# DeltaNet's q, k and v projection as seven products of halves, with weight sums by GpSimd during attention and operands streamed from DRAM

## The reference

```
def encoder_layer(x, ...):
    h = rms_norm(x, norm1_g)
    proj = h @ w_in
    q_lat, kv_lat, k_rope, qkv, z, a_f, a_b, b_f, b_b = split_cols(proj, SPLITS)
    mla_out = mla_mixer(q_lat, kv_lat, k_rope, ...)
    gdn_out = gdn_mixer(qkv, z, a_f, a_b, b_f, b_b, ...)
    x = x + jnp.concatenate([mla_out, gdn_out], axis=-1) @ w_o
    x = x + ec_moe(rms_norm(x, norm2_g), w_router, w_gate, w_up, w_down)

def gdn_mixer(qkv, z, ...):
    qkv = jax.nn.silu(centred_depthwise_conv(qkv, conv_w))      # 5 taps
    q, k, v = split_cols(qkv, (1024, 1024, 1024))               # 8 heads of 128 each
    q = l2_normalize(q); k = l2_normalize(k)
    ...                                                         # chunked delta rule, forward and backward
```

## Time and profile before

| | |
|---|---|
| median of 3 runs | 2980.59 us (2979.1 to 2981.39) |
| the profiled execution, its own time | 2983.76 us |
| its span in the trace | 2982.0 us |
| TensorE busy | 2801.7 us, 94% |
| VectorE, ScalarE, GpSimd busy | 1092.2, 609.8, 601.6 us |
| DMA | 603.95 MB, 203 GB/s on average |

### The profile page before, as it was taken

One profiled execution on the slowest core, in us unless ns is written; L12 is line 12 of the kernel. 1 busy time (PEld: TensorE's weight loads), 2 busy tenths in 40 slices (PEclk: granted clock), 3 DMA queues, 4 the chain that ended last, 5 costly groups with the idle time before them and its releaser, 6 DMA issues. The chain is left out here.

```text
span 2982.0 us, 53948 instructions
## 1 busy us (share of the span) xinstructions
PE 2801.7 (94%) x19063; PEld 1404.3 (47%) x19063; DVE 1092.2 (37%) x2185; ACT 609.8 (20%) x1806; POOL 601.6 (20%) x969
## 2 busy tenths in 40 slices
PE   8999999999999999999788999999999999999997
PEld 4544455555666666566465455432223232322232
DVE  1145444421674575476675434411111111111100
ACT  4100455412213312311411010321111111111100
POOL 1444111104214222320530000212111111112111
PEclk9999999999999999999899999999999999999999
DMA  6664100021111110200413637799999999999996
GB/s 241 220 219 132 53 29 29 11 94 57 57 44 50 44 57 24 70 23 26 147 44 146 235 141 261 290 424 408 376 400 385 398 390 398 395 387 394 378 412 216
DMA packets 170388, 603.95 MB, mean 203 GB/s; under 512 B 16527, under 2 KB 81895, under 8 KB 116455
## 3 DMA queue, kind: packets, MB, share of 16 engines
q1 hardware_dynamic: 163175, 587.58, 51.4%
q0 software_dynamic: 6912, 12.59, 2.4%
HBM read 554.14 MB, written 45.98 MB: 201 GB/s over the span
## 5 line engine op out<-in xcount | busy, mean ns | idle before, releaser
L2727 PE MATMUL psum<-wbuf 128*32 128x512 f32 x2976 | 334.9, 606 | 24.7 <-issue 22.9
L1444 PE MATMUL psum<-xT,wbuf 128*128 128x512 f32 x720 | 342.0, 613 | 0.3 <-PEq L828 0.3
L2727 PE MATMUL psum<-x,wbuf 128*32 128x512 f32 x3024 | 330.1, 592 | 0.0
L715 POOL COPY wbuf<-xT 128x16 f32 x533 | 114.4, 215 | 759.9 <-issue 433.5
L2727 PEld LDWEIGHTS psum<-wbuf 128*32 128x32 f32 x2976 | 98.4, 112 | 255.9 <-issue 255.9
L715 DVE COPY wbuf<-xT 128x16 f32 x500 | 94.4, 190 | 337.2 <-issue 336.3
L2727 PEld LDWEIGHTS psum<-x,wbuf 128*32 128x32 f32 x3024 | 99.2, 110 | 225.3 <-issue 225.3
L1444 PEld LDWEIGHTS psum<-xT,wbuf 128*128 128x128 f32 x720 | 133.3, 194 | 127.4 <-issue 122.4
L2745 PE MATMUL psum<-x,hT 128*32 128x512 f32 x1584 | 173.3, 593 | 13.9 <-DVE hT L2808 13.2
L715 ACT COPY wbuf<-xT 128x16 f32 x503 | 111.2, 221 | 276.5 <-issue 273.9
L1447 PE MATMUL psum<-xT,wbuf 128*128 128x256 f32 x736 | 164.9, 379 | 0.0
(11 more groups left out here) (330 smaller groups left out, 3694.4 us busy)
## 6 DMA issues: line engine op xcount, KB each, us to landing
x<-in_w_down SPq DMA_DIRECT2D x66, 1024.0 KB, 11.0
wbuf<-in_w_gate SPq DMA_DIRECT2D x65, 1024.0 KB, 10.3
wbuf<-in_w_up SPq DMA_DIRECT2D x65, 1024.0 KB, 12.9
x<-in_w_gate SPq DMA_DIRECT2D x63, 1024.0 KB, 8.0
x<-in_w_up SPq DMA_DIRECT2D x63, 1024.0 KB, 10.6
wbuf<-in_w_down SPq DMA_DIRECT2D x62, 1024.0 KB, 11.7
wbuf<-in_w_in SPq DMA_DIRECT2D x16, 2048.0 KB, 8.9
wbuf<-weight_sums SPq DMA_DIRECT2D x16, 2048.0 KB, 9.4
```

The costliest lines, as they stand in the source:

```text
L715: last = copy(k.xeT[:, half, :, t:t + 1], k.mixT[:, :, cols][:, :, bass.ds(r, 1)])
L1444: last = nc.tensor.matmul(ps[:, b, 0:SS_], wg[:, m % 2, d, h * P:(h + 1) * P], k.xT[:, d, SP_:T], start=(d == 0), stop=(d == KD - 1))
L2727: last = nc.tensor.matmul(ps[32 * j:32 * j + 32, g, :].rearrange("p (x n) -> p x n", x=2), xeT[:, half, q, 32 * g:32 * g + 32], m[:, :, kk ...
```

## The change

The three kinds (k, q, v) of a pair of heads become one unit of work ("kind"): two heads side by side, two halves of the tokens (384 each) and two halves of the width. Instead of 8 block products, 7 are made (Strassen's scheme). Each product has 8 steps of 384 tokens. A pair needs 21 products, 168 steps; the four pairs need 84 products, 672 steps.

* The four sums of weights per kind are formed by GpSimd in the attention block, in 48 units of three subtractions, and stored to DRAM (`qkv_weight_sums`). The four sums of tokens fall out of the z products of the first block and are stored there (`token_operands`).
* In DeltaNet the weights of a product are loaded six products ahead into six slots, and the token operands into three slots of `xT` (a fourth, A22, stays). Six of seven products need a fresh token operand of 1.5 MB, which is issued when the product that used the slot before is done.
* Products land in two PSUM banks in turn. ScalarE copies the first product of each kind out (`keep`), VectorE adds the six others into `pre` (`add`), with one or two blocks each.
* The convolution of a kind can begin when its seventh product is added; v is the last kind of a pair.
* In attention the last pair gets two steps a tile, and three products in all, in place of 40 steps.
* The z tiles are paired 0 with 3, 1 with 4, 2 with 5, and `xT` is laid out by halves of the tokens.

The core of the diff:

```
+TYPES = (1, 0, 2)
+PRODUCT_ORDER = (1, 6, 2, 7, 5, 4, 3)
+TOKENS_OF = {1: A11, 2: A12, 3: S4, 4: A22, 5: S1, 6: S2, 7: S3}
+W_SLOTS = 6
+IN_ATTENTION = 3 * HK
+def product_step(k, p, d):
+    v, _ = TOKEN_AT[p]
+    last = k.nc.tensor.matmul(k.psum[:, product_bank(p), 0:SIDE], k.w_slot[p % W_SLOTS][:, d, :],
+                              k.x_slot[v].rearrange("p (k t) -> p k t", k=HK)[:, d, :],
+                              start=(d == 0), stop=(d == HK - 1))
...
@@ attention, SyncE @@
+                def comb_load(u):
+                    n, kp = divmod(u, 4)
+                    if u >= 2:
+                        sp.wait_ge(s_cs[u % 2], cs_base + 16 * (u // 2))
+                    c0 = C_QKV + TYPES[n % 3] * GW + n // 3 * 2 * P
+                    for g in range(2):
+                        k0 = HK * g + 2 * kp
+                        src = a["w_in"][0].rearrange("(p k) n -> p k n", k=KD)[:, k0:k0 + 2, c0:c0 + 2 * P]
+                        for h in range(2):
+                            sp.dma_start(w_comb[u % 2][:, 2 * g + h], src[:, :, h * P:(h + 1) * P]).then_inc(s_cl[u % 2], 16)
+                def comb_store(lo, hi):
+                    for u in range(lo, hi):
+                        n, kp = divmod(u, 4)
+                        if u + 1 < N_COMB:
+                            comb_load(u + 1)
+                        sp.wait_ge(s_comb, comb_base + 3 * u + 3)
+                        sp.dma_start(k.wsum[n, :, :, 2 * P * kp:2 * P * (kp + 1)].rearrange("m p c -> p m c"),
+                                     w_comb[u % 2].rearrange("p m k c -> p m (k c)")).then_inc(s_cs[u % 2], 16)
+                UNITS_TO = ((5, 10, 18), (18, 23, 32), (32, 36, 44), (44, 44, N_COMB))
@@ attention, GpSimd @@
+                combine(0, 5)
                 for i in range(HP):
                     pool.wait_ge(s_sq, i * NT + NT)
...
                     nc.gpsimd.tensor_tensor(qrot[..., HALF:], tmp[:, 0], tmp[:, 1], ALU.add).then_inc(s_qr, 1)
                     pool.wait_ge(s_qr, i + 1)
+                    combine(*((5, 13), (13, 27), (27, 41), (41, N_COMB))[i])
@@ attention, TensorE @@
-                        first_qkv(3 * u, 3 * u + 3)
+                        products(min(2 * u, 2 * HK), min(2 * u + 2, 2 * HK))
@@ DeltaNet, SyncE @@
+                def refill(lo, hi):
+                    for p in range(lo, hi):
+                        if p + W_SLOTS >= N_PROD and p not in TOKEN_LOADS:
+                            continue
+                        sp.wait_ge(s_prod, PROD_BASE + p + 1)
+                        for v, o in TOKEN_LOADS.get(p, ()):
+                            load_tokens(k, sp, v, o)
+                        if p + W_SLOTS < N_PROD:
+                            load_weights(k, sp, p + W_SLOTS)
...
                     if i + 1 == HP:
-                        sp.wait_ge(s_proj, HP * NC)
+                        sp.wait_ge(s_prod, PROD_BASE + N_PROD)
+                        for n in (KINDS - 2, KINDS - 1):
+                            convolved(sp, n)
                         sp.dma_start(k.mixT[:, 0:H], k.mix[0:H].rearrange("h p t -> p h t")).then_inc(k.s_mix, 16)
@@ DeltaNet, TensorE @@
-                project(0, 1, SECOND)
-                for c in range(2, NC):
-                    project(0, c)
+                project(21 * HK - IN_ATTENTION)
...
-                            project(i + 1, c, at, at + a)
+                            project(a)
...
-                            project(i + 1, c, at + a, at + a + b)
+                            project(b)
...
-                        project(i + 1, 4, LV * sum(IN_LEVEL[2]),
-                                between={12: lambda: scan(i, 4, 0), 14: lambda: scan(i, 4, 1), 16: lambda: scan(i, 4, 2),
-                                         20: lambda: scan(i, 5, 0), 24: lambda: scan(i, 5, 1), 28: lambda: scan(i, 5, 2)})
-                        steps = {6: lambda: output(i)}
+                        project(28 - LV * sum(IN_LEVEL[2]),
+                                {0: lambda: scan(i, 4, 0), 2: lambda: scan(i, 4, 1), 4: lambda: scan(i, 4, 2),
+                                 7: lambda: scan(i, 5, 0), 10: lambda: scan(i, 5, 1), 13: lambda: scan(i, 5, 2)})
+                        steps = {12: lambda: output(i)}
...
-                        project(i + 1, 5, between=steps)
+                        project(28, steps)
@@ DeltaNet, VectorE @@
+                def add(p):
+                    n, m, q = product_of(p)
+                    dve.wait_ge(s_prod, PROD_BASE + p + 1)
+                    jobs = {6: [(kept, c21)], 2: [(c11, c21)], 7: [(c21, kept)], 5: [(c22, c21), (kept, kept)],
+                            4: [(c21, c21)], 3: [(c12, kept)]}[q]
+                    for to, of in jobs:
+                        for cols, o in to:
+                            last = nc.vector.tensor_tensor(o, ps[:, product_bank(p), cols], of[0][1][:, cols], ALU.add)
@@ DeltaNet, GpSimd @@
-                    pool.wait_ge(s_pre, m + 1)
+                    pool.wait_ge(s_ea, scalar_to(7 * kind + 6))
+                    pool.wait_ge(s_ev, vector_to(7 * kind + 6))
```

More of the change, by code:

```diff
@@ L349, in _ @@
                 comb_store(13, 18)
+                sum_store(S4, 0)
                 load_w(3)
@@ L1996, in _ @@
                                 copy_part(2)
+                        if more and r < 2:
+                            add(p0 + (8, 11)[r])
                         if r < 2:
```

459 lines of the change are left out of this document (301 added, 158 removed).

## The result

The changed kernel takes 3055.03 us (median of 4 runs, 3047.12 to 3058.71) against 2980.99 us before: ratio 1.0246, 95% interval 1.0233 to 1.0258. It is 74 us slower. The forecast was 3056 us in a range of 2992 to 3100.

What follows compares the result with a forecast made beforehand. TensorE, busy for 94% of the span, was taken to bound the kernel; 47 + (9 - 3.4) - 15 + 35 + 1 + 2 = 75.6 us, set against 2980.6, gave 3056 us, with a range of 2992 to 3100.

Steps and rivals of the forecast that it cites:

- The gain on TensorE: Projection steps: 62.0 us gross, as 12.0 in attention, 3.4 in the first projection and 46.3 in three pairs.
- What of the 46.3 is left: Three full DeltaNet pairs: 5.0 us a pair kept after waits and VectorE's additions, 15 in all, bounds 0 and 25.
- the pair's start: Start of each DeltaNet pair: 56 steps save 5.2 us, 2.0 kept because the third sum of squares waits for ScalarE.
- The additions: VectorE adding products in the DeltaNet pairs: up to 18 us a pair, 3 of it counted on the chain.
- DeltaNet's first step: Fourth product waits for S3, loaded only after the barrier behind 1.0 MB of weights: cost 9 us, bounds 6 and 13.
- The weight sums in attention: GpSimd's units, 6.2 us each, make rotations late: attention grows by 47 us net of the 12.0 gain, bounds 21 and 68.
- The rotations: Attention: rotations 0 and 1 late by about 2 us each, 2 and 3 by 26 each; sum 56, bounds 33 and 72.
- The clock: Three long waits let TensorE's clock fall, and it starts again at 1.2 of 2.4 GHz: 2 us, bounds 0 and 5.
- The last pair: Loads of `mix` and output weights wait for GpSimd's v convolution, TensorE waits 40 us: cost 35, bounds 28 and 38.
- The first block: Token sums must be stored before VectorE forms the next; the last store leaves product 6 late: 1 us, bounds 0 and 4.
- The stream: Rival: token and weight operands bind DeltaNet's products, adding 20 us, or 60 with worse queueing: 3076 to 3116; chance 0.05.
- The faster rival: Both queues keep up, under 4.6 us a unit and last pair covered: 2962, or 2925 if filling counts in full; chance 0.12.

Runs made afterwards that it cites:

- experiment 6: Changed kernel with VectorE adding only 8 columns of each block in place of up to 384; 3044.06 us, ratio 1.0222.
- experiment 2: Changed kernel with all 48 weight-sum units left out, products needing a sum reading a plain block of weights; 3004.29 us, ratio 1.0087.
- experiment 9: Changed kernel with early last-pair loads, three unit buffers, new rotation cuts and SyncE stops, S3 loaded in attention, reordered squares; 2956.2 us, ratio 0.9916.
- experiment 5: Changed kernel with each DeltaNet token operand load bringing only 128 of 3072 columns; 3042.04 us, ratio 1.0216.
- experiments 9 and 10: The second of these: experiment 9's kernel with S1 early too, product 1's weights ahead of the store of mix, later sums of squares; 2943.73 us, ratio 0.9877.

## Why the prediction was right, and where only its sum was

The sum was +75.6 us, the profiled execution has +74.8. Both large mechanisms were right and shown by taking each away. Its parts were less exact than the sum:

* **The gain on TensorE** (62.0 gross). Attention without units is 12.8 us shorter (12.0). From the first step to the last pair TensorE's busy time fell by 41.0 where 3.4 + 46.3 = 49.7 were taken out. The granted clock is 0.97 against 0.98; one hundredth of 734 us is 7, an estimate, so it can hold most of the missing 8.7, but which rows they are was not counted.
* **What of the 46.3 is left.** From the first sum of squares to the last pair the stretch fell from 716.5 to 700.3 us, 16.2 less, where 15 were forecast. That near agreement is partly luck: in the five other profiles with the same DeltaNet code this stretch takes 696.2 to 709.7 us, 7 to 20 less. By its pieces: the waits at the rounds' products grew from 15.8 to 27.3 us, of 24.3 of filling saved, so about half was kept and not a third. The output transposes' waits fell by 7.0 (8.3 to 1.3), so the pair's end kept its saving. The step that failed is the pair's start: I kept 2.0 of 5.2 there, and the waits for the third sum of squares grew from 2.5 to 19.5 us in all, which ate all of it. The worst one, 9.15, stands where the last pair's sums come ahead of the pair, behind VectorE's addition of product 20 and the second convolution of q; I had looked only at the first sort. The additions, forecast at 9, cost 5.5 us by the waits of experiment 6 and 10.3 by its window, which the spread of the runs leaves open.
* **DeltaNet's first step**: the wait is 10.6 (9 forecast, bounds 6 and 13). With the clock behind it (23.37 - 20.64 = 2.7) and 1.8 of issue the stage, 3.4 us of work less, grew by 10.7 in place of 5.6 (101.9 to 112.6).
* **The weight sums in attention** (+47, bounds 21 and 68): +36.8. Against experiment 2 it is 39.8 of waits and 9.8 of TensorE's busy time, less the 12.8. The mis-sized term is the unit's pitch. I took 6.2 us; it is 5.2 undisturbed and 78.0 / 14 = 5.6 in a lap. The issue of four loads takes 1.91 us, not 2.4, and the store has landed 3.2 us after its issue (393.13 to the next load at 396.35), not 4.3. By rows alone the lower bound, 5.5, was the better choice. *The Trainium skill*, page "DMA: Bandwidth & Descriptors", section "Anatomy of one DMA — SWDGE (gpsimd) path", gives about 2.0 us plus the bytes at 436 GB/s for a DMA that GpSimd issues. The prediction used it without that condition for a store of 512 KB that SyncE issues, an estimate of 3.2 us; this trace agrees, with 3.2. The rotations cost 42.9 us and not 56, of which 9.2 fell on rotations 0 and 1, where I had 4: SyncE's stop ahead of `wqkv` was in the order of its queue, and I did not follow it. The 3 us for a slower VectorE came to 1: its 326 operations took 143.4 us against 135.7 without the units, but the waits for its probabilities are 9.4 us against 8.4. The high bound of 72 for the rotations adds up to 70.
* **The clock** was a term of 2 us with a bound of 5, and it was sized too low. TensorE's busy time in attention is 9.8 us over that of experiment 2 (and 4.6 to 15.7 over it in the five other profiles of the same attention). Not all of it comes from the long waits: 5.9 are left in experiment 9, where no rotation is waited for and the granted clock is 0.98. With the 2.7 at DeltaNet's first step it makes up for most of the 13 us that the rotations had too much.
* **The last pair** (+35, bounds 28 and 38): +31.6. The loads start 33.8 us after the transposes of k begin (1512.21 - 1478.44; 35.5 forecast), land 27.1 later, and the wait is 38.78 (40 forecast). Here each step was right.
* **The first block** (+1, bounds 0 and 4): +11.9 in the profiled execution, outside the bounds, and -1.9 to +1.8 in the eleven others with the same code. The place was the forecast's own, the store of the sums behind the output units; that SyncE can come to it 11 us late was not in it. How often that happens is open; the changed kernel's runs lie between 3047 and 3059, and which of them had it was not seen. Without it the profiled one would be 3047.
* **The rivals.** The stream does not bind (experiment 5). The faster rival asked for less than 4.6 us a unit and the last pair covered: it is what experiments 9 and 10 bring about, 2956 and 2944, where it gave 2962 and down to 2925.

So the text "two waits of 16 to 33 us" was right for rotations 2 and 3 only at its low end (18.2 and 15.6), and part of the agreement of the sum is luck: -10 in attention against +11 in the first block.

## What to carry to other kernels

Work given to an idle engine is not free because its busy share is low: count what stands ahead of the engine's next due piece in its own queue, in the queue of the engine that loads for it, and what that queue stops at. When a buffer's neighbour becomes the reason for a wait, ask of each load whether its own bytes touch it: three of four loads had waited 34 us for nothing. And when TensorE's waits are counted, add what the clock takes behind each.

## What the runs showed of the hardware that was not expected

* The clock behind short waits. After waits of 7.2 to 18.2 us the transposes of `qrot` run at the lower of TensorE's two levels, 1.2 GHz of 2.4 (granted 0.50 between 520 and 530 us), six in 1.51 us where the six of `kraw` take 0.82. The same wait of 3.44 us at a sum of squares was followed once by a pair of rows of 2.05 us (granted 0.50) and twice by one of 1.23 and 1.25 (0.84 and 0.81), in place of 1.02; behind 1.69 us the granted clock stayed at 1.00. In attention the 950 instructions took 283.1 us at a granted clock of 0.91 against 273.3 at 0.99.
* Four loads of 128 KB took SyncE 1.91 us, 0.48 each, when they were issued behind a store that had landed. The two loads of a unit in the first block took 0.60 each. With a third buffer, when a store or loads had just been issued, four took 2.6, and so did the four in the changed kernel that followed the load of `wqkv` (2.67 at 416.82).
* Executions of one and the same changed kernel lie 11 us apart (3047.12 to 3058.71), those of the kernel before 2.6 in as many runs and 7.4 in seven.
